# Operands of the top-k moved from SBUF to PSUM banks, and the place numbers of both token blocks made at once

## The chip, the cores and the metric

The kernel runs on one core of one Trainium2 chip. The metric is the device time of one launch in microseconds, the median of three runs. A profiled execution of the same program gives the trace that is read here. A core has five engines: TensorE (PE in the profile, its weight loads PEld), VectorE (DVE), ScalarE (ACT), GpSimd (POOL) and SyncE (SP), which here issues the transfers. On-chip memory is SBUF and, as TensorE's output, PSUM (8 banks of 512 float32 per partition).

## The reference

Two layers of an encoder trunk on 256 tokens of 1024 channels, float32. Each layer adds a mixed branch (attention, Hyena convolutions, FNet) and then a product-key expert branch, `x = x + peer(rmsnorm(x))`. The change lies in the expert branch:

```python
def peer(x, w_query, sub_keys, u_tab, v_tab):
    q = (xt @ w_query).reshape(T, PEER_HEADS, 2, PEER_DK // 2)           # T=256, 8 heads
    s = jnp.einsum('thpd,phkd->thpk', q, sub_keys)                       # 128 keys a side
    s_top, i_top = lax.top_k(s, PEER_TOPK)                               # 16 of 128, both sides
    cand = (s_top[:, :, 0, :, None] + s_top[:, :, 1, None, :]).reshape(T, 8, 256)
    cand_idx = (i_top[:, :, 0, :, None] * 128 + i_top[:, :, 1, None, :]).reshape(T, 8, 256)
    best, pos = lax.top_k(cand, PEER_TOPK)                               # 16 of 256
    idx = jnp.take_along_axis(cand_idx, pos, axis=-1)
    g = jax.nn.softmax(best, axis=-1)
    ...
    a = gelu(einsum('thkd,td->thk', u_tab[idx], xb))
    out = einsum('thk,thkd->td', g * a, v_tab[idx])
```

## The kernel before

The kernel doesn't gather experts. It multiplies all 16384 rows of the table u with the tokens (128 tiles of 128 experts), takes gelu, weighs the result by a gate matrix built from the picks, and multiplies it with all of the table v. Each layer runs in a loop over `l`; each engine has its own program, and the engines meet by semaphores (`Signal`, `at`).

Products are made in three parts for precision: each 128 x 1024 tile lands in `raw` (4 slots), ScalarE writes its rounded high part `tab_hi` and another engine the low part, `tab_lo = raw - tab_hi`, half a tile (128 x 512) at a time. `tab_hi` and `tab_lo` have two tile slots, four halves. A half may be written when TensorE has counted in `half_used` that it is through with the half two tiles earlier. TensorE's `u_tile` (L820 to L822) makes 12 matmuls of 256 columns for a half: high by x_lo, high by x_hi, low by x_hi, for 4 blocks of 128.

Who makes the low parts is written out by stages. For u tiles 0 to 39 it is GpSimd (`EARLY = 40`, `u_lower` in its program, L1264), since VectorE is then in the top-k. Tiles 40 to 47 are VectorE's (`u_lower_half`, L1592), in program order behind the top-k. When tile 47 is multiplied, TensorE waits for `topk_done`, transposes the picks (L868), waits for VectorE's copies of them (L1604 to L1606) and goes on with the stage of tiles 48 to 111, where the gates are built (L1611 to L1623) and GpSimd again makes the low parts. Behind `topk_done` GpSimd also sets parts of `work` to one (L1269 to L1278).

The top-k on VectorE, with tokens on the partitions and two token blocks `b` of 128:
- `top16` (L1543 to L1547) takes the 16 largest of a row in five passes: for the 16 rows (8 heads, 2 sides) of each block, giving `v_top` and `i_top`; L1555 turns the indices to float.
- For each block the candidate sums `cand` (L1558) of 16 x 16 for 8 heads, 2048 elements, and `top16` over them, giving `best` and `pos`.
- L1566 and L1567 subtract the largest from `best` (`best_done`), and ScalarE takes its exponential (L1118, `gate_exp`) at a place of its own order.
- For each block the place numbers: `pos >> 4` and `pos & 15` (L1571, L1572), turned to float (L1573), 128 elements for each of two sides. For each side the key look-up, each of 128 picks x 16 ranks = 2048 elements: compare with 0 to 15 (L1575), multiply by the key indices (L1580), sum over the ranks (L1581).
- After `gate_exp` the sum, the reciprocal and the product (L1583 to L1585, `topk_done`).

All these arrays lie in SBUF: `cand`, `eq` and `scores` in `work`, the others in `onehot`, `small` and `kc`. `link` lets VectorE wait for the instruction it wraps (`dve_step`, of which `DVE_STEPS` are counted in a layer), and `settled` drains the engine.

While this runs, TensorE writes PSUM banks 0 and 1 and ScalarE reads them (gelu). The picks' transposes go to banks 4 and 5.

Of the kernel before, what the change touches and what calls it, by code (L numbers as in the profile page):

```python
# [5 lines left out]
ALU = mybir.AluOpType  # L6
# [4 lines left out]
U32 = mybir.dt.uint32  # L11

P = 128
# [11 lines left out]
PH, KEYS, TOPK = 8, 128, 16  # L25
HP = 2 * PH
PICKS = PH * TOPK
# [38 lines left out]
QUERY_T = 0  # L66
UNIT_A = SPEC + 2048
SUBKEYS = SPEC
CAND, EQ, SCORES = 24576, 26624, 28672


A0, B0, O0, Q0, U0, V0, TILES = 0, 8, 16, 24, 40, 168, 296
# [7 lines left out]

FNET_BANKS, HYENA_BANKS, ATTN_BANKS = ((6, 7), (0, 2)), ((1, 4), (5, 3)), ((6, 7), (0, 2))
FNET_SUMS, HYENA_SUMS, ATTN_SUMS = 2, 4, 2
DVE_STEPS = 55
PARAM_MATS, PARAM_PIECES, DFT_PIECES = 2, 5, 6
FOLLOWING = 1 + PARAM_PIECES + DFT_PIECES + 1

# [8 lines left out]
def at(signal, layer, count):  # L95

    return signal.sem, layer * signal.per_layer + count


def hybrid_encoder(nc, x_in, w_proj, sub_keys, tab_u, tab_v, pvec, pmat, gain_qk, kconst, cfilter,  # L100
                   cdft, final_g, out):
    with ExitStack() as ctx:
# [3 lines left out]
        def sig(name, per_layer):  # L106
            return Signal(ctx.enter_context(nc.semaphore(name)), per_layer)
# [18 lines left out]
        ps = ctx.enter_context(nc.psum_tensor("ps", [P, 8, 512], F32))  # L126

        workf = work[:, :, :].rearrange("p j t -> p (j t)")
        onef = onehot[:, :, :, :, :].rearrange("p s a t c -> p (s a t c)")
# [3 lines left out]
        def area(start, n):  # L133
            return workf[:, start:start + n]
# [74 lines left out]
        subk = area(SUBKEYS, HP * KEYS).rearrange("p (k n) -> p k n", k=HP)  # L209
        scores = area(SCORES, TB * HP * KEYS).rearrange("p (b k n) -> p b k n", b=TB, k=HP)  # L210
        cand = area(CAND, PH * TOPK * TOPK).rearrange("p (h a b) -> p h a b", h=PH, a=TOPK)
        eq = area(EQ, PICKS * TOPK).rearrange("p (n r) -> p n r", r=TOPK)
        v_top = onef[:, 0:512].rearrange("p (b k n) -> p b k n", b=TB, k=HP)
        i_top = onef[:, 512:1024].bitcast(U32).rearrange("p (b k n) -> p b k n", b=TB, k=HP)
        i_topf = onef[:, 1024:1536].rearrange("p (b k n) -> p b k n", b=TB, k=HP)
        best = onef[:, 1536:1792].rearrange("p (b h n) -> p b h n", b=TB, h=PH)
        pos = onef[:, 1792:2048].bitcast(U32).rearrange("p (b n) -> p b n", b=TB)
        minus_j = chosenf[:, 0:SEQ]
        place_u = onef[:, 0:256].bitcast(U32).rearrange("p (s n) -> p s n", s=2)
        place_f = onef[:, 256:512].rearrange("p (s n) -> p s n", s=2)  # L220


        const_in = sig("const_in", 0)
# [11 lines left out]
        half_used = sig("half_used", 2 * TILES)  # L235
        dve_step = sig("dve_step", DVE_STEPS)
        mlp_ready = sig("mlp_ready", 2)
# [87 lines left out]
        def settled(eng):  # L325

            eng.drain()
# [958 lines left out]
        def _(dve):  # L1286
            v = nc.vector
# [4 lines left out]
            with dve.Fori(0, DEPTH) as l:  # L1292
                count = [0]

                def link(ins):

                    count[0] += 1
                    ins.then_inc(dve_step.sem, 1)
                    dve.wait_ge(*at(dve_step, l, count[0]))
# [240 lines left out]
                def top16(values, indices, row, rows):  # L1540


                    steps = (lambda r: v.max(values(r)[:, 0:8], row(r)),  # L1543
                             lambda r: v.max_index(indices(r)[:, 0:8], values(r)[:, 0:8], row(r)),
                             lambda r: v.match_replace(row(r), values(r)[:, 0:8], row(r), NEG),
                             lambda r: v.max(values(r)[:, 8:16], row(r)),
                             lambda r: v.max_index(indices(r)[:, 8:16], values(r)[:, 8:16], row(r)))  # L1547
                    for step in steps:
                        for r in range(rows):
                            last = step(r)  # L1550
                        settled(dve)

                for b in range(TB):
                    top16(lambda r: v_top[:, b, r, :], lambda r: i_top[:, b, r, :], lambda r: scores[:, b, r, :], HP)
                link(v.tensor_copy(i_topf, i_top))  # L1555
                for b in range(TB):
                    side = v_top[:, b, :, :].rearrange("p (h s) n -> p h s n", s=2)
                    v.tensor_tensor(  # L1558
                        cand, side[:, :, 0, :].rearrange("p h (n a) -> p h n a", a=1).broadcast_to([P, PH, 16, 16]),
                        side[:, :, 1:2, :].broadcast_to([P, PH, 16, 16]), ALU.add)  # L1560
                    settled(dve)
                    top16(lambda r: best[:, b, r, :], lambda r: pos[:, b, r * 16:(r + 1) * 16],
                          lambda r: cand[:, r, :, :].rearrange("p a b -> p (a b)"), PH)
# [3 lines left out]
                v.tensor_tensor(bests, bests, ssg.rearrange("p (n a) -> p n a", a=1).broadcast_to([P, 16, 16]),  # L1567
                                ALU.subtract).then_inc(best_done.sem, 1)

                for b in range(TB):  # L1570
                    link(v.tensor_single_scalar(place_u[:, 0, :], pos[:, b, :], 4, op=ALU.logical_shift_right))  # L1571
                    link(v.tensor_single_scalar(place_u[:, 1, :], pos[:, b, :], 15, op=ALU.bitwise_and))  # L1572
                    link(v.tensor_copy(place_f, place_u))  # L1573
                    for s in range(2):
                        link(v.tensor_tensor(  # L1575
                            eq, place_f[:, s, :].rearrange("p (n a) -> p n a", a=1).broadcast_to([P, PICKS, TOPK]),
                            iota16.rearrange("p (a n) -> p a n", a=1).broadcast_to([P, PICKS, TOPK]), ALU.is_equal))
                        side = i_topf[:, b, :, :].rearrange("p (h s) n -> p h s n", s=2)[:, :, s:s + 1, :]
                        eq4 = eq.rearrange("p (h k) r -> p h k r", h=PH)
                        link(v.tensor_tensor(eq4, eq4, side.broadcast_to([P, PH, TOPK, TOPK]), ALU.mult))  # L1580
                        link(v.tensor_reduce(chosen[:, s, b, :], eq, AX.X, ALU.add))  # L1581
# [247 lines left out]
```

## Time and profile before

| | us |
|---|---|
| median of 3 runs | 2042.25 (2041.79 to 2042.98) |
| profiled execution | 2039.95 |
| its span, first to last instruction | 2038.1 |
| TensorE busy (PE) | 1952.9 |
| VectorE busy (DVE) | 1320.5 |
| ScalarE busy (ACT) | 1103.7 |
| GpSimd busy (POOL) | 769.7 |

The busy time of an engine is an average over stages with different limits, so it says little of a change in one stage. Times in the views count from the span's start. In a timeline neighbouring instructions of one line are merged: the first number is the start, the second the time from the first start to the last end, xN the count. "out<-in" names the buffers; a bracket tells how long the engine was idle before and who released it. TensorE's matmuls overlap, so a single one is shown longer than the distance to its neighbour.

### The profile page before, as it was taken

The page shows a single profiled execution, that of the slowest core. Times are in us where ns is not written, and L with a number is a line of the kernel's source. Part 1 is how long each engine was busy: PE and PEld are TensorE (multiplying, and loading weights), DVE is VectorE, ACT ScalarE, POOL GpSimd, SP SyncE. Part 2 cuts the span into 40 slices and gives each one's busy share as a digit, 9 for nine tenths or more (in the row PEclk, how much of TensorE's full clock was granted, in tenths as well). Part 3 has the DMA queues.
Part 4 walks back from the last instruction along what each step waited for, and adds up shares of the span by engine and source line. Part 5 has one row for each costly group of instructions (what it writes and reads, how often), then busy time and mean ns, then how long its engine had stood idle before and what let it go on. Part 6 is the DMA issues. An engine that isn't in the chain of part 4 may idle for free.

```text
span 2038.1 us, 43068 instructions
## 1 busy us (share of the span) xinstructions
PE 1952.9 (96%) x12792; PEld 1782.5 (87%) x12792; DVE 1320.5 (65%) x2869; ACT 1103.7 (54%) x2124; POOL 769.7 (38%) x553
## 2 busy tenths in 40 slices
PE   7989998999999999999998999989999999999997
PEld 5779997999999888888777799979999998888886
DVE  4655699566666666666547557986666666666665
ACT  4344454666664555555533454546666555555554
POOL 4433599567770000000064416995767600000000
PEclk9989999999999999999989999999999999999999
DMA  6215454544445567555522154544444456665555
GB/s 210 74 42 172 151 184 138 162 137 141 137 140 172 186 208 246 196 192 191 184 74 83 55 183 148 183 144 145 144 134 144 134 175 196 226 227 194 196 192 179
DMA packets 93499, 327.09 MB, mean 160 GB/s; under 512 B 10736, under 2 KB 11504, under 8 KB 93168
## 3 DMA queue, kind: packets, MB, share of 16 engines
q1 hardware_dynamic: 93424, 326.18, 49.1%
q8 instruction: 36, 0.59, 0.1%
q14 instruction: 39, 0.32, 0.0%
HBM read 325.09 MB, written 1.05 MB: 160 GB/s over the span
## 4 chain that ended last, share of the span: by engine, by line
PE 89%; DVE 5%; issue 3%; POOL 2%; ACT 1%; DMA 0%; DVEq 0%; POOLq 0%; SPq 0%; ACTq 0%
PE ps L820 12%; PE ps L821 12%; PE ps L822 12%; PE ps L893 11%; PE ps L895 11%; PE ps L896 11%; PE ps L839 6%; PE ps L793 2%; PE ps L796 2%; PE ps L795 2%; POOL tab_lo L1264 1%; DVE work L1370 1%; PE ps L604 1%; PE ps L570 1%; PE ps L523 1%
## 5 line engine op out<-in xcount | busy, mean ns | idle before, releaser
L1264 POOL TENSOR_TENSOR tab_lo<-raw,tab_hi 128x512 fp32r<-128x512 f32 x416 | 585.9, 1422 | 262.5 <-ACT tab_hi L1096 181.6
L820 PE MATMUL ps<-x_lo,tab_hi 128*128 128x256 f32 x2048 | 591.8, 289 | 22.2 <-POOL tab_lo L1264 18.9
L822 PE MATMUL ps<-x_hi,tab_lo 128*128 128x256 f32 x2048 | 579.1, 283 | 0.0
L821 PE MATMUL ps<-x_hi,tab_hi 128*128 128x256 f32 x2048 | 579.0, 283 | 0.0
L1677 DVE TENSOR_TENSOR tab_lo<-raw,tab_hi 128x512 fp32r<-128x512 f32 x512 | 354.4, 692 | 268.7 <-ACT tab_hi L1191 265.3
L1096 ACT ACTIVATE tab_hi<-raw 128x512 fp32r<-128x512 f32 x504 | 317.6, 631 | 339.0 <-PE ps L822 334.5
L820 PEld LDWEIGHTS ps<-x_lo,tab_hi 128*128 128x128 f32 x2048 | 392.1, 191 | 25.7 <-POOL tab_lo L1264 25.5
L893 PE MATMUL ps<-tab_lo,w_hi 128*128 128x512 f32 x1024 | 398.6, 389 | 0.9 <-DVE w_lo L1685 0.9
L896 PE MATMUL ps<-tab_hi,w_lo 128*128 128x512 f32 x1024 | 398.4, 389 | 0.0
L895 PE MATMUL ps<-tab_hi,w_hi 128*128 128x512 f32 x1024 | 398.4, 389 | 0.0
L821 PEld LDWEIGHTS ps<-x_hi,tab_hi 128*128 128x128 f32 x2048 | 392.6, 192 | 0.0
L822 PEld LDWEIGHTS ps<-x_hi,tab_lo 128*128 128x128 f32 x2048 | 392.0, 191 | 0.0
L1191 ACT ACTIVATE tab_hi<-raw 128x512 fp32r<-128x512 f32 x512 | 319.3, 624 | 89.8 <-PE ps L896 89.0
L893 PEld LDWEIGHTS ps<-tab_lo,w_hi 128*128 128x128 f32 x1024 | 192.2, 188 | 41.8 <-DVE tab_lo L1677 1.7
L896 PEld LDWEIGHTS ps<-tab_hi,w_lo 128*128 128x128 f32 x1024 | 192.2, 188 | 39.7
L895 PEld LDWEIGHTS ps<-tab_hi,w_hi 128*128 128x128 f32 x1024 | 192.2, 188 | 39.7
L1181 ACT ACTIVATE w_hi<-work 128x256 fp32r (+1 forms) x256 | 106.8, 417 | 201.7 <-PE ps L896 200.3
L1623 DVE TENSOR_TENSOR work<-ps,work 128x512 f32 (+1 forms) x128 | 88.5, 692 | 157.4 <-PE ps L839 157.4
L1212 POOL TENSOR_TENSOR small<-small,kc 128x2 f32<-128x2 f32 x10 | 6.9, 691 | 445.8 <-DVE small L1304 428.6
L920 ACT ACTIVATE tab_hi<-raw 128x512 fp32r<-128x512 f32 (+1 forms) x168 | 100.3, 609 | 130.6 <-PE ps L796 47.3
L1611 DVE TENSOR_SCALAR onehot<-kc,picks 128x128 f32<-128x128 f32 x512 | 168.1, 389 | 0.6
L1219 POOL TENSOR_TENSOR tab_lo<-raw,tab_hi 128x512 fp32r<-128x512 f32 (+1 forms) x96 | 121.4, 1277 | 116.9 <-ACT tab_hi L920 115.5
(204 smaller groups left out, 2524.8 us busy)
## 6 DMA issues: line engine op xcount, KB each, us to landing
raw<-tab_u SPq DMA_DIRECT2D x256, 512.0 KB, 3.3
raw<-tab_v SPq DMA_DIRECT2D x256, 512.0 KB, 3.3
raw<-w_proj SPq DMA_DIRECT2D x68, 512.0 KB, 3.6
raw<-w_proj SPq DMA_DIRECT2D x16, 384.0 KB, 3.2
work<-cdft SPq DMA_DIRECT2D x18, 256.0 KB, 3.8
work<-cfilter SPq DMA_DIRECT2D x9, 256.0 KB, 4.3
work<-sub_keys SPq DMA_DIRECT2D x2, 1024.0 KB, 6.5
work<-pmat SPq DMA_DIRECT2D x6, 304.0 KB, 4.4
```

What stands on the lines that cost most here:

```text
L820: mm(bank, hi, x_lo[:, 4 * h + k, :], start=(h + k == 0), stop=False)
L821: mm(bank, hi, x_hi[:, 4 * h + k, :], start=False, stop=False)
L822: last = mm(bank, lo, x_hi[:, 4 * h + k, :], start=False, stop=(h + k == 4))
L839: last = mm(ps[:, 2 + s, t * P:(t + 1) * P], onehot[:, s % 2, 0, t, :], onehot[:, s % 2, 1, t, :], start=True, stop=True)
L893: mm(bank, w_hi[:, s % 2, tok], lo, start=(first and s == 0), stop=False, skip_group_check=True)
L895: mm(bank, w_hi[:, s % 2, tok], hi, start=False, stop=False, skip_group_check=True)
L896: last = mm(bank, w_lo[:, s % 2, tok], hi, start=False, stop=last_tile, skip_group_check=True)
L1096: fn(half(tab_hi, s, h), half(raw, s, h), ACT.Copy).then_inc(hi_done.sem, 1)
L1191: fn(half(tab_hi, s, h), half(raw, s, h), ACT.Copy).then_inc(hi_done.sem, 1)
L1264: tt(half(tab_lo, s, h), half(raw, s, h), half(tab_hi, s, h).bitcast(F32), ALU.subtract).then_inc(lo_pool.sem, 1)
L1611: last = v.tensor_scalar(onehot[:, slot, 0, t, :], iota, picks[:, 0, bass.ds(n * 4 + t, 1)], picks[:, 2, bass.ds(n * 4 + t, 1)], ALU.is_eq ...
L1677: v.tensor_tensor(half(tab_lo, s, h), half(raw, s, h), half(tab_hi, s, h).bitcast(F32), ALU.subtract).then_inc(lo_dve.sem, 1)
```

## The change

The `eq` array leaves SBUF for PSUM banks 4 to 7 (2048 float32), so that the compare writes it there, the multiply reads and writes it there, and the reduce reads it there. The float place numbers `place_f` lie in bank 3, and are made for both blocks at once: one shift, one mask, each of 256 elements, and one conversion of 512, in place of two rounds of 128, 128 and 256. `place_u` takes 512 words of `onehot`, where `v_top` lay. A new copy puts the first side's 16 best key scores of all heads and blocks, 256 elements, in bank 2 (`v_first`), and the candidate sums read them from there, the other side from SBUF. `DVE_STEPS` goes from 55 to 51.

```diff
-CAND, EQ, SCORES = 24576, 26624, 28672
+CAND, SCORES = 24576, 28672
-DVE_STEPS = 55
+DVE_STEPS = 51
-        eq = area(EQ, PICKS * TOPK).rearrange("p (n r) -> p n r", r=TOPK)
-        place_u = onef[:, 0:256].bitcast(U32).rearrange("p (s n) -> p s n", s=2)
-        place_f = onef[:, 256:512].rearrange("p (s n) -> p s n", s=2)
+        posf = onef[:, 1792:2048].bitcast(U32)
+        place_u = onef[:, 0:512].bitcast(U32).rearrange("p (s n) -> p s n", s=2)
+
+        v_first = ps[:, 2, 0:256].rearrange("p (m n) -> p m n", n=TOPK)
+        place_f = ps[:, 3, :].rearrange("p (s n) -> p s n", s=2)
+        eq = ps[:, 4:8, :].rearrange("p k c -> p (k c)").rearrange("p (n r) -> p n r", r=TOPK)
...
+                v.tensor_copy(v_first, v_top.rearrange("p b (h s) n -> p s (b h) n", s=2)[:, 0, :, :])
                 link(v.tensor_copy(i_topf, i_top))
                 for b in range(TB):
                     side = v_top[:, b, :, :].rearrange("p (h s) n -> p h s n", s=2)
                     v.tensor_tensor(
-                        cand, side[:, :, 0, :].rearrange("p h (n a) -> p h n a", a=1).broadcast_to([P, PH, 16, 16]),
-                        side[:, :, 1:2, :].broadcast_to([P, PH, 16, 16]), ALU.add)
+                        cand, v_first[:, b * PH:(b + 1) * PH, :].rearrange("p h (n a) -> p h n a", a=1)
+                        .broadcast_to([P, PH, 16, 16]), side[:, :, 1:2, :].broadcast_to([P, PH, 16, 16]), ALU.add)
...
+                v.tensor_single_scalar(place_u[:, 0, :], posf, 4, op=ALU.logical_shift_right)
+                link(v.tensor_single_scalar(place_u[:, 1, :], posf, 15, op=ALU.bitwise_and))
+                link(v.tensor_copy(place_f, place_u))
                 for b in range(TB):
-                    link(v.tensor_single_scalar(place_u[:, 0, :], pos[:, b, :], 4, op=ALU.logical_shift_right))
-                    link(v.tensor_single_scalar(place_u[:, 1, :], pos[:, b, :], 15, op=ALU.bitwise_and))
-                    link(v.tensor_copy(place_f, place_u))
                     for s in range(2):
+                        place = place_f[:, s, b * PICKS:(b + 1) * PICKS]
                         link(v.tensor_tensor(
-                            eq, place_f[:, s, :].rearrange("p (n a) -> p n a", a=1).broadcast_to([P, PICKS, TOPK]),
+                            eq, place.rearrange("p (n a) -> p n a", a=1).broadcast_to([P, PICKS, TOPK]),
                             iota16.rearrange("p (a n) -> p a n", a=1).broadcast_to([P, PICKS, TOPK]), ALU.is_equal))
                         side = i_topf[:, b, :, :].rearrange("p (h s) n -> p h s n", s=2)[:, :, s:s + 1, :]
                         eq4 = eq.rearrange("p (h k) r -> p h k r", h=PH)
                         link(v.tensor_tensor(eq4, eq4, side.broadcast_to([P, PH, TOPK, TOPK]), ALU.mult))
                         link(v.tensor_reduce(chosen[:, s, b, :], eq, AX.X, ALU.add))
```

## Rows read from the trace of the kernel before

**Rows 1.** The page: the chain that ended last, shares of the span.
```profile
PE 89%; DVE 5%; issue 3%; POOL 2%; ACT 1%; DMA 0%; DVEq 0%; POOLq 0%; SPq 0%; ACTq 0%
```

**Rows 2.** GpSimd's line L1264: durations in ns; who waited, us, times.
```profile
L1264 POOL TENSOR_TENSOR tab_lo<-raw,tab_hi x416: 1264/1296/3320, 216.3 to 1623.8; 128x512 fp32r<-128x512 f32 x139
...
  PE ps L820: 18.9, 14
```

**Rows 3.** Busy by stretch: length, engines' busy us (instructions), clock, DMA share, GB/s.
```profile
228.00:300.00 72.00, 72.00 (x601) 71.89 (x601) 69.39 (x361) 38.57 (x63) 65.38 (x48) 1.00 0.50 166
300.00:314.00 14.00, 14.00 (x119) 14.00 (x118) 13.64 (x35) 7.29 (x12) 13.46 (x11) 1.00 0.60 200
314.00:352.00 38.00, 28.55 (x225) 27.13 (x224) 37.41 (x18) 16.76 (x27) 38.00 (x19) 1.00 0.36 115
352.00:377.50 25.50, 25.50 (x214) 25.50 (x214) 11.70 (x17) 13.10 (x22) 14.45 (x7) 1.00 0.63 199
```

**Rows 4.** Timeline of TensorE: the stage's first product and end, both layers.
```profile
227.75 0.36 PE L820 MATMUL ps<-x_lo,tab_hi 128*128 128x256 f32 x1
...
377.52 0.82 PE L868 MATMUL ps<-kc,chosen 128*128 128x128 f32 x6
...
1237.93 0.36 PE L820 MATMUL ps<-x_lo,tab_hi 128*128 128x256 f32 x1
...
1387.68 0.82 PE L868 MATMUL ps<-kc,chosen 128*128 128x128 f32 x6
```

**Rows 5.** Timeline of VectorE, first layer: place numbers, first compare, end of top-k.
```profile
308.37 1.32 DVE L1571 TENSOR_SCALAR onehot<-onehot 128x128 uint32<-128x128 uint32 x1
...
311.31 3.27 DVE L1575 TENSOR_TENSOR work<-onehot,kc 128x2048 f32<-128x2048 f32 x1
...
329.29 1.36 DVE L1571 TENSOR_SCALAR onehot<-onehot 128x128 uint32<-128x128 uint32 x1
...
333.27 3.27 DVE L1575 TENSOR_TENSOR work<-onehot,kc 128x2048 f32<-128x2048 f32 x1
...
351.98 0.81 DVE L1585 TENSOR_TENSOR chosen<-onehot,small 128x256 f32<-128x256 f32 x1
353.30 2.73 DVE L1592 TENSOR_TENSOR tab_lo<-raw,tab_hi 128x512 fp32r<-128x512 f32 x4 [0.50 <-PE ps L822]
...
384.03 0.69 DVE L1623 TENSOR_TENSOR work<-ps,work 128x512 f32<-128x512 f32 x1 [1.46 <-PE ps L839]
```

**Rows 6.** Timeline of GpSimd: beside a compare, a reduce and a gate's product.
```profile
312.42 3.30 POOL L1264 TENSOR_TENSOR tab_lo<-raw,tab_hi 128x512 fp32r<-128x512 f32 x1
...
318.96 1.30 POOL L1264 TENSOR_TENSOR tab_lo<-raw,tab_hi 128x512 fp32r<-128x512 f32 x1
...
383.61 1.29 POOL L1264 TENSOR_TENSOR tab_lo<-raw,tab_hi 128x512 fp32r<-128x512 f32 x1 [3.92 <-ACT tab_hi L1096]
```

**Rows 7.** VectorE's groups by line and shape: busy us, mean ns, idle before.
```profile
L1623 DVE TENSOR_TENSOR work<-ps,work 128x512 f32 x112 | 77.4, 691 | 140.4 <-PE ps L839 140.4
L1575 DVE TENSOR_TENSOR work<-onehot,kc 128x2048 f32<-128x2048 f32 x8 | 26.8, 3350 | 0.3
L1580 DVE TENSOR_TENSOR work<-work,onehot 128x2048 f32<-128x2048 f32 x8 | 26.0, 3248 | 0.3
...
L1581 DVE TENSOR_REDUCE chosen<-work 128x128 f32<-128x2048 f32 x8 | 18.3, 2286 | 0.3
...
L1558 DVE TENSOR_TENSOR work<-onehot 128x2048 f32<-128x2048 f32 x4 | 12.5, 3123 | 0.2
...
L1699 DVE TENSOR_TENSOR x<-ps,x 128x1024 f32<-128x1024 f32 x4 | 4.9, 1224 | 4.2 <-PE ps L896 4.0
```

**Rows 8.** Timeline of ScalarE: the exponential of the best scores.
```profile
317.02 0.42 ACT L1118 ACTIVATE onehot<-onehot 128x256 f32<-128x256 f32 x1
```

**Rows 9.** ScalarE's groups by line and shape: gelu in place and into SBUF.
```profile
L1127 ACT ACTIVATE ps<-ps 128x512 f32<-128x512 f32 x80 | 46.4, 580 | 3.9 <-PE ps L822 3.9
...
L1100 ACT ACTIVATE work<-ps 128x512 f32 x40 | 23.2, 579 | 0.0
```

## The prediction

> **What bounds the kernel now.** I began with the page's shares of the chain that ended last: TensorE holds 89% of it and VectorE 5% [rows 1]. So a shorter VectorE stretch is worth nothing in itself; it counts only where TensorE stands still because of it. The view of GpSimd's line L1264, which makes the low part of a half tile, shows that TensorE's first product of a half (L820) waited for it for 18.9 us in 14 places, although the median half takes GpSimd only 1.296 us [rows 2]. The longest takes 3.320 us. That gap is the thing to explain. GpSimd's name for this in the page is POOL, VectorE's DVE.
>
> The table by stretch says where it sits. From 228 to 314 us TensorE starts 601 + 119 matmuls in 86 us, one each 0.12 us. From 314 to 352 us it starts 225 in 38 us, where 317 would fit at that pace; then it is at pace again [rows 3]. The granted clock is 1.00 (the 2.4 GHz level) in all four stretches, so the missing 92 matmuls (11.0 us) are no matter of the clock. The whole stage of the first 48 table tiles is 48 x 2 halves x 12 = 1152 matmuls, 138.24 us at 0.12. It starts at 227.75 and the transposes behind it start at 377.52, that is 149.77 us: 11.5 us lost. The second layer has the same from 1237.93 to 1387.68, 149.75 us [rows 4]. The waits account for 18.9 / 2 = 9.5 us of it in a layer; the rest fits the product that comes first after a stop, which takes 0.36 us where in the stream one follows the other by 0.12 [rows 2, 4].
>
> The timelines of VectorE and GpSimd side by side say why. In just this stretch, from 311.31 us on, VectorE runs the key look-up: compare (L1575) 3.35 us in the mean, multiply (L1580) 3.25, reduce (L1581) 2.29, each four times a layer [rows 5, 7]. GpSimd's half that meets the first compare takes 3.30 us (there are eight like it in a layer, one for each compare and multiply), the one beside the first reduce 1.30 us [rows 6]. The reduce streams the same 2048 elements, from one SBUF operand, in 2286 ns [rows 7]. So the two engines do not merely share the memory: an instruction of VectorE with two SBUF operands and one of GpSimd take turns. A compare is 1 us of waiting for GpSimd's half to end and 2.3 us of own work, in which GpSimd stands, 3.30 - 1.28 = 2.02 us. Eight of those per layer are 16.2 us of GpSimd, of which TensorE feels 11.5; some 4.7 us go into the up to four halves that GpSimd may be ahead, and into its 0.15 us of reserve per half (1.29 against TensorE's 12 x 0.12 = 1.44). The two candidate sums of a layer (L1558, 3.12 us in the mean) do the same earlier, before 300 us, and TensorE loses nothing there, by the count above [rows 3, 7].
>
> **The part of GpSimd.** After the change compare, multiply and candidate sum each have one operand in PSUM and one in SBUF. The nearest row for that is the gate's product (L1623, one PSUM operand, one in SBUF): at 384.03 us it runs for 0.69 us inside a GpSimd half of 1.29 us, and neither is longer for it; in 112 of them the mean is 691 ns [rows 5 to 7]. The chance that a two-operand instruction with a PSUM operand no longer takes turns rests on that row and on the reduce. Then GpSimd needs 1.26 to 1.30 us a half against 1.44, and TensorE keeps its pace [rows 2]. Worth per layer: up to 11.5 us, of which I leave 0.2 for the longer first product and small delays: 11.3. The page "SBUF — State Buffer" of the Trainium skill, section "Who interferes with whom", says the same: two SBUF inputs contend with a GpSimd instruction that reads SBUF, at most one does not; by it too the whole wait would go.
>
> **The part of VectorE, and the cover.** TensorE's tiles 40 to 47 are lowered by VectorE, in its program behind the top-k. If GpSimd stops being late, this is what is late next. TensorE would ask for tile 40's first half at 227.75 + 80 x 1.44 + 0.1 = 343.0 us. Now the top-k ends at 351.98 + 0.81 = 352.8 and the first lowered half is there at 353.30 + 2.73 / 4 = 354.0, 1.2 us after [rows 5]. So the top-k has to end by 341.8: 11.0 us sooner than now, or TensorE only changes what it waits for. The sum for one layer:
> - Candidate sums: 2 x 3.12 become 2 x 2.29. The price of 2048 elements with one PSUM operand is from 691 ns for 512 (L1623) and 1224 for 1024 (L1699), so 1.04 ns an element and 2.29 us; equal to the SBUF reduce. Saves 1.67. Added is the copy of 256 key scores to PSUM, 0.691 - 256 x 0.00104 = 0.42 us. Net 1.2 [rows 7].
> - Place numbers: now two rounds, from 308.37 to 311.31 and from 329.29 to 333.27, 6.9 us. After: one shift and one mask of 256 elements and one copy of 512 into PSUM. A shift of 128 elements takes 1.32 us, where 128 at 1.04 ns with the fixed part of 0.16 would be 0.3: mostly turns with GpSimd, which I keep, 2 x 1.3; a copy of 512 with a PSUM operand takes 0.69. Together 3.3, so it saves 3.6 (2.7 if all three are 1.4, 5.4 if the shifts meet nothing) [rows 5, 7].
> - Compares: 4 x 3.35 = 13.4 become 9.2: 4.2. Multiplies: 4 x 3.25 = 13.0 become 9.2: 3.8. Reduces: 2.29 from SBUF, 2.29 by the slope from PSUM: unchanged [rows 7].
>
> In all 12.9 us: the top-k ends at 339.9, 1.9 us before it must. ScalarE's exponential, for which VectorE waits before its last three instructions, is done at 317.02 + 0.42 = 317.4 and hangs on ScalarE's own place in the order [rows 8]. The raw tiles arrive while TensorE is at pace (166 to 200 GB/s), so the pace asks of the DMA queues what they already do [rows 3]. GpSimd's setting of ones follows the top-k and ends earlier by as much.
>
> What no row shows is VectorE writing to PSUM: compare, multiply and two copies now do. Lower bound is the SBUF price, 2.29 us. The nearest row of a write is ScalarE's, whose gelu from PSUM takes 580 ns in place (L1127) against 579 into SBUF (L1100) [rows 9]. The dearest that I can argue is that the multiply and compare take two passes, 4.4 us each (2 x 2.13 + 0.15). I take 2.29, the row nearest. The page "VectorE: DVE Perf Modes", section on the TRN2 errata, speaks against the change: 120 cycles of fixed cost from PSUM against 58 from SBUF. The trace does not have it: 512 elements take 691 ns with a PSUM operand (L1623) and 2.73 / 4 = 0.68 us with SBUF operands alone (L1592) [rows 5, 7]. By the page, at 65 ns in each of some 16 instructions, the top-k would end 1.0 us later, at 340.9, still in time, with half the margin: the sum would not move, and rival 1 would be twice as near.
>
> **The sum.** 2 layers x 11.3 = 22.6 us. The profiled execution took 2039.95 us (span 2038.1); it would take 2017.35 (span 2015.5). The median of the runs is 2.3 above the profiled one, so the median goes from 2042.25 to 2019.65. Nothing behind the stage gives it back: the gate stage begins when the picks are transposed, on TensorE's time, and everything after is a chain of its own.
>
> **The rivals.**
> 1. VectorE is late at tile 40. It decides from the point where the eight compares and multiplies take 1.9 / 8 = 0.24 us more than 2.29. At the present 3.3 us each (no gain in length, but no turns for GpSimd either), the top-k ends 8.1 us later, TensorE waits 6.2 of it and 2 x 5.1 remain: 2032. For it: the margin is thin, and no row shows such a write. Against it: ScalarE's row.
> 2. The other side, slower. If a read and a write of PSUM by the same instruction take two passes (4.4 us), the top-k ends 8 x 2.1 = 16.9 us later, TensorE stands at tile 40 for 15.0 us, and loses 15.0 - 11.3 = 3.7 us a layer: 2049.6. From 2.29 + (1.9 + 11.3) / 8 = 3.94 us per instruction the change is a loss. Against it: L1127, in place.
> 3. Half of the turns stay (the multiplies, say, since they read and write the same tensor). GpSimd stands 8.1 us a layer, 4.7 of it are absorbed as now, 3.4 reach TensorE, and 2 x 7.9 are won: 2026.5.
> 4. The change does not do what it says: GpSimd stands as long as now, for a reason other than the second SBUF operand. Then the place numbers still get shorter, on an engine that isn't waited for: 2042. Against it: the reduce and L1623.
>
> **How the numbers follow.** Forecast 0.74, 2018.5 to 2021.5 by itself. Rivals 1 and 3, which end between 2022 and 2036, 0.15 together. Rival 4, 0.06. Rival 2, 0.05. The range reaches from 2017.0 (all of the 11.5 us, and some spread of the runs) to 2029.0, which takes in rival 3 and rival 1 up to 3.1 us an instruction. A measurement of this kernel can tell about 0.2% (4 us) from no change: faster 0.89, same 0.06, slower 0.05.
>
> **What the profile after would show.** L1264's longest half on GpSimd under 2 us and no wait of TensorE for it; about 0.12 us per matmul through the whole stage, and 138.5 to 139 us from its first product to the transposes. Compare, multiply and candidate sum near 2.29 us each; the top-k's last instruction near 340 us. If the compares are longer than 2.6 us and TensorE waits for VectorE's lowering at tile 40, rival 1 or 2 is at work; if GpSimd still shows halves of 3.3 us, rival 3 or 4. The prediction is wrong if a write to PSUM by VectorE has a price of its own or if a PSUM operand doesn't end the turns.

## The result, and the profile after

The changed kernel takes 2019.55 us (median of 4 runs, 2018.87 to 2020.94) against 2042.02 for the kernel before measured beside it: ratio 0.9893, 95% interval 0.9879 to 0.9907. The forecast was 2019.65. The profiled execution took 2020.94 us, its span is 2019.0 (2038.1 before).

The busy table by stretch of the changed kernel, over the same stage as [rows 3] (start and end of the stretch, its length, the busy us and instruction counts of PE, PEld, DVE, ACT and POOL, granted clock, share and GB/s of the transfers):

```profile
230.00:302.00 72.00, 72.00 (x602) 72.00 (x602) 69.71 (x365) 38.58 (x64) 63.14 (x49) 1.00 0.52 169
302.00:316.00 14.00, 14.00 (x119) 14.00 (x119) 13.69 (x31) 6.95 (x12) 12.77 (x11) 1.00 0.55 186
316.00:354.00 38.00, 38.00 (x319) 38.00 (x318) 32.02 (x23) 22.99 (x37) 33.19 (x21) 1.00 0.56 186
354.00:368.00 14.00, 14.00 (x119) 14.00 (x118) 4.85 (x7) 6.89 (x13) 3.43 (x3) 1.00 0.52 171
```

The third stretch is the one that matters: 319 matmuls in 38 us where there were 225 (a count in brackets takes in every instruction that lies in the stretch with any part, so it is a little higher than the number of starts). GpSimd, which had no free moment in those 38 us, is now busy for 33.2. The timeline of TensorE gives the stage's length, to be set against [rows 4]:

```profile
229.38 0.36 PE L823 MATMUL ps<-x_lo,tab_hi 128*128 128x256 f32 x1
...
367.69 0.49 PE L871 MATMUL ps<-kc,chosen 128*128 128x128 f32 x3
...
1230.23 0.36 PE L823 MATMUL ps<-x_lo,tab_hi 128*128 128x256 f32 x1
...
1368.54 0.82 PE L871 MATMUL ps<-kc,chosen 128*128 128x128 f32 x6
```

138.31 us in either layer, against 149.77 and 149.75, and 138.24 for 1152 matmuls at 0.12. So nothing is left to win in this stage without fewer or shorter matmuls. GpSimd's line (durations in ns, lowest, median, longest; then who waited, us, times) is now L1267, and no product of TensorE waits for it, only two weight loads (PEld):

```profile
L1267 POOL TENSOR_TENSOR tab_lo<-raw,tab_hi x416: 1264/1296/1799, 217.9 to 1604.6; 128x512 fp32r<-128x512 f32 x139
...
  PEld ps L823: 3.7, 2
```

The median is that of [rows 2] and the longest fell from 3320 to 1799 ns. VectorE's groups by shape (xcount, busy us, mean ns), for [rows 7]:

```profile
L1580 DVE TENSOR_TENSOR ps<-ps,kc 128x2048 f32<-128x2048 f32 x8 | 18.4, 2300 | 0.3
L1585 DVE TENSOR_TENSOR ps<-ps,onehot 128x2048 f32<-128x2048 f32 x8 | 18.4, 2299 | 0.3
L1586 DVE TENSOR_REDUCE chosen<-ps 128x128 f32<-128x2048 f32 x8 | 18.3, 2291 | 0.3
...
L1562 DVE TENSOR_TENSOR work<-ps,onehot 128x2048 f32<-128x2048 f32 x4 | 9.2, 2291 | 0.2
```

and its timeline from the index conversion to the first lowered half of tile 40, for [rows 5]:

```profile
270.66 0.43 DVE L1558 COPY ps<-onehot 128x256 f32<-128x256 f32 x1
271.00 1.26 DVE L1559 CAST onehot<-onehot 128x512 f32<-128x512 uint32 x1
...
309.82 1.39 DVE L1574 TENSOR_SCALAR onehot<-onehot 128x256 uint32<-128x256 uint32 x1
...
313.27 2.30 DVE L1580 TENSOR_TENSOR ps<-ps,kc 128x2048 f32<-128x2048 f32 x1
...
341.99 0.42 DVE L1590 TENSOR_TENSOR chosen<-onehot,small 128x256 f32<-128x256 f32 x1
342.92 1.90 DVE L1597 TENSOR_TENSOR tab_lo<-raw,tab_hi 128x512 fp32r<-128x512 f32 x3 [0.50 <-ACT tab_hi L1099]
```

From the stage's first product to the end of the top-k it was 352.79 - 227.75 = 125.0 us; now it is 342.41 - 229.38 = 113.0. The first half of tile 40 is there at 342.92 + 1.90 / 3 = 343.55, and TensorE asks for it, by its pace of 1.44 us a half, at 229.38 + 80 x 1.44 + 0.1 = 344.7: a margin of 1.1 us.

### The profile page after: what moved, and what is told of

It is laid out like the page before. It is cut to its first block, busy times and chain, and to the rows that moved or that the text cites. A ratio compares the mean times of both kernels' runs of the same rounds, so it can differ in the third digit from the quotient of the medians.

```text
span 2019.0 us, 43056 instructions
## 1 busy us (share of the span) xinstructions
PE 1950.9 (97%) x12792; PEld 1783.7 (88%) x12792; DVE 1299.6 (64%) x2865; ACT 1103.6 (55%) x2124; POOL 736.6 (36%) x553
## 4 chain that ended last, share of the span: by engine, by line
PE 91%; DVE 4%; issue 2%; ACT 1%; DMA 0%; POOL 0%; DVEq 0%; POOLq 0%; SPq 0%; ACTq 0%
PE ps L823 12%; PE ps L824 12%; PE ps L825 12%; PE ps L898 11%; PE ps L896 11%; PE ps L899 11%; PE ps L842 6%; PE ps L796 2%; PE ps L799 2%; PE ps L798 2%; DVE work L1373 1%; PE ps L607 1%; PE ps L573 1%; PE ps L526 1%; PE ps L528 1%
## 5 line engine op out<-in xcount | busy, mean ns | idle before, releaser
L1267 POOL TENSOR_TENSOR tab_lo<-raw,tab_hi 128x512 fp32r<-128x512 f32 x416 | 552.5, 1337 | 270.9 <-ACT tab_hi L1099 183.2
```

Source lines behind the costliest of these rows:

```text
L1267: tt(half(tab_lo, s, h), half(raw, s, h), half(tab_hi, s, h).bitcast(F32), ALU.subtract).then_inc(lo_pool.sem, 1)
```

## The experiments

The theory: VectorE's instructions with two SBUF inputs and GpSimd's take turns, TensorE loses what GpSimd is late, and the end of the top-k has to stay ahead of tile 40. Four kernels take the change apart, two load the cover, and the rest carry the step to other places; one run repeats the changed kernel beside them. "Stage" is TensorE's time from the first product of the 48 tiles to the transposes, read as above.

**The place numbers alone**, all operands in SBUF (added to the kernel before):

```diff
+        place_u = onef[:, 0:512].bitcast(U32).rearrange("p (s n) -> p s n", s=2)
+        place_f = area(CAND, 512).rearrange("p (s n) -> p s n", s=2)
...
+                v.tensor_single_scalar(place_u[:, 0, :], posf, 4, op=ALU.logical_shift_right)
+                link(v.tensor_single_scalar(place_u[:, 1, :], posf, 15, op=ALU.bitwise_and))
+                link(v.tensor_copy(place_f, place_u))
                 for b in range(TB):
-                    link(v.tensor_single_scalar(place_u[:, 0, :], pos[:, b, :], 4, op=ALU.logical_shift_right))
...
```

> The kernel before with the place numbers of both blocks made at once, every operand left in SBUF. Theory (GpSimd is held up by VectorE's instructions with two SBUF inputs, and TensorE by GpSimd): the compares and multiplies still hold GpSimd eight times a layer, so the stage of the first 48 tiles still takes 149.7 us and the time stays at 2042 us (2040.5 to 2043.5), although the top-k ends some 3.5 us sooner. Rival (it is the length of VectorE's work that counts): 3.5 us a layer won, 2035 us.

Measured: 2043.8 us, ratio 1.0008 (0.9999 to 1.0018), stage 150.1 us. That is 0.3 us above the range and far from the rival's 2035. The top-k ended 2.5 us sooner after the stage's start (350.95 - 228.44 = 122.5 us, where some 3.5 sooner was expected), and it was worth nothing. The group of the compare and the wait of TensorE for GpSimd (us, times, longest) are as before the change:

```profile
L1577 DVE TENSOR_TENSOR work<-work,kc 128x2048 f32<-128x2048 f32 x8 | 27.1, 3386 | 0.3
```
```profile
PE ps L821 <- POOL tab_lo L1265: 19.7, 14, 1.6
```

So VectorE's length was not what bound the stage.

**The PSUM operands alone**, the place numbers made per block again (in the changed kernel):

```diff
-                v.tensor_single_scalar(place_u[:, 0, :], posf, 4, op=ALU.logical_shift_right)
...
+                for b in range(TB):
+                    link(v.tensor_single_scalar(place_u[:, 0, :], pos[:, b, :], 4, op=ALU.logical_shift_right))
```

> The changed kernel with the place numbers made block by block again, the operands in PSUM kept. Theory: GpSimd is free of VectorE, no half above 2 us; the top-k ends about 2.6 to 3.6 us later than in the changed kernel, where the first half of tile 40 was there 1.1 us before TensorE asked, so TensorE waits 1.5 to 2.5 us per layer for VectorE's lowering at tile 40: 2022.5 to 2024.5 us. Rival (the place numbers are of no account once GpSimd is free): 2019.5 us.

Measured: 2023.11 us (2020.55 to 2023.39), ratio 0.9905 (0.9888 to 0.9922), stage 139.5 us. A new wait is there, small and once a layer, for VectorE's low part of tile 40:

```profile
PE ps L822 <- DVE tab_lo L1595: 1.8, 2, 0.9
```

The top-k ended at 344.75 - 229.65 = 115.1 us after the stage's start, 2.1 later than in the changed kernel (2.6 to 3.6 were expected); less the margin of 1.1 this is 1.0, and the stage is 1.2 longer. The two stages explain 2.4 us; that the medians lie 3.6 apart is not explained by them, and the two intervals overlap. The place numbers are worth something only because the PSUM operands are there.

**Input or output?** Two kernels each leave one of the look-up's two long instructions with two SBUF inputs. In the first `eq` is back in SBUF: the compare reads PSUM and writes SBUF. In the second only the place numbers are: the compare reads SBUF twice and writes PSUM.

```diff
-        eq = ps[:, 4:8, :].rearrange("p k c -> p (k c)").rearrange("p (n r) -> p n r", r=TOPK)
+        eq = area(26624, PICKS * TOPK).rearrange("p (n r) -> p n r", r=TOPK)
```

> The changed kernel with the array eq back in SBUF: the compare still reads its place numbers from PSUM but writes to SBUF, the multiply has two SBUF inputs again. Theory (the second SBUF input holds GpSimd): compares 2.29 us and no hold, multiplies 3.25 us and four halves of 3.3 us per layer; TensorE loses about 3.4 us a layer, 2026.5 us (2024 to 2029). Rival (it is the output in SBUF that holds GpSimd): compares hold it too, eight halves of 3.3 us, near 2042 us.

```diff
-        place_f = ps[:, 3, :].rearrange("p (s n) -> p s n", s=2)
+        place_f = area(CAND, 512).rearrange("p (s n) -> p s n", s=2)
```

> The changed kernel with the float place numbers back in SBUF: the compare has two SBUF inputs but still writes to PSUM, the multiply is as changed. Theory (inputs decide): compares 3.3 us and four halves of 3.3 us per layer, multiplies 2.30 us without a hold; TensorE loses about 3.4 us a layer, 2026.5 us (2024 to 2029). Rival (the output decides): no long half, 2019.5 us.

Measured: 2026.93 us (ratio 0.9929, 0.9910 to 0.9948) and 2026.80 us (0.9925, 0.9908 to 0.9941), stages 142.1 and 142.1 us. VectorE's groups, first of the one with `eq` in SBUF, then of the one with the place numbers there:

```profile
L1585 DVE TENSOR_TENSOR work<-work,onehot 128x2048 f32<-128x2048 f32 x8 | 20.6, 2579 | 0.3
L1580 DVE TENSOR_TENSOR work<-ps,kc 128x2048 f32<-128x2048 f32 x8 | 18.3, 2291 | 0.3
```
```profile
L1580 DVE TENSOR_TENSOR ps<-work,kc 128x2048 f32<-128x2048 f32 x8 | 20.7, 2590 | 0.3
L1585 DVE TENSOR_TENSOR ps<-ps,onehot 128x2048 f32<-128x2048 f32 x8 | 18.4, 2299 | 0.3
```

Of these two-operand instructions it doesn't matter which it is, nor where it writes: the one with two SBUF inputs is held, the one with one is not. GpSimd's longest half is 3325 and 3326 ns in these kernels. That is half of the turns for a third of the loss (3.8 us of 11.5 a layer); the sum of the prediction, in which GpSimd's lead takes up 4.7 us of standing, gives 3.4. The held instruction is at 2.58 us in the mean shorter than before the change (3.25). With `eq` in SBUF the first multiply of a layer takes 3.16 us and the other three 2.38 to 2.40: these begin when a GpSimd half is nearly over, and wait 0.1 us. GpSimd has four long halves in the layer all the same, of 3.16 to 3.33 us.

The second of these kernels also answers the question for a short instruction with one SBUF input, the conversion of the place numbers. In both rows here it begins 0.1 us behind the start of a GpSimd half; first the changed kernel, which writes to PSUM, then the one that writes to SBUF:

```profile
312.54 0.70 DVE L1576 CAST ps<-onehot 128x512 f32<-128x512 uint32 x1
```
```profile
312.86 1.48 DVE L1576 CAST work<-onehot 128x512 f32<-128x512 uint32 x1
```

Here the output decides: written to PSUM it doesn't wait, written to SBUF it waits for the half's end (314.05 us) and is done 0.3 us after it.

**The candidate sums back in SBUF**, with the copy left out:

```diff
-                v.tensor_copy(v_first, v_top.rearrange("p b (h s) n -> p s (b h) n", s=2)[:, 0, :, :])
...
-                        cand, v_first[:, b * PH:(b + 1) * PH, :].rearrange("p h (n a) -> p h n a", a=1)
+                        cand, side[:, :, 0, :].rearrange("p h (n a) -> p h n a", a=1)
```

> The changed kernel with the candidate sums reading both operands from SBUF again, without the copy to PSUM. Theory: each sum holds one GpSimd half at 3.1 to 3.3 us, twice a layer near 272 and 290 us, which GpSimd's lead takes up, so TensorE does not wait for it; the top-k ends 0.4 to 1.3 us later, against a margin of 1.1 us at tile 40. Stage 138.3 to 138.6 us, time 2019.5 to 2020.5 us. Rival (every hold reaches TensorE in part): 0.7 of 2 x 2 us a layer, 2025 us.

Measured: 2019.96 us, ratio 0.9891 (0.9876 to 0.9906), stage 138.48 us. GpSimd has a half of 3.29 and one of 3.15 us beside the sums, and TensorE doesn't feel them. The top-k ends 340.88 - 227.68 = 113.2 us after the stage's start, 0.2 later than in the changed kernel: the third part of the change shortens VectorE by 0.2 us, and is worth nothing that can be measured, as [rows 3] already said of the sums.

**The cover, loaded.** Three, and in another kernel two, more compares in the changed kernel, which have one operand in PSUM and change no value:

```diff
+                        for _ in range(4 if b + s == 2 else 1):
...
```

> The changed kernel with the third compare of the key look-up made four times, which changes no value: three more instructions of 2.33 us a layer that have one operand in PSUM. Theory (TensorE needs the top-k's end at tile 40, and GpSimd is not held by these): 7.0 us more of VectorE, less the margin of 1.1, is 5.9 us of waiting for VectorE's lowering per layer, stage 144.2 us, time 2031.3 us (2030 to 2033), no GpSimd half above 2 us. Rival (the end of the top-k is covered by more than the margin that I read): below 2026 us.

> The changed kernel with the third compare made three times: two more instructions of 2.33 us a layer. With three more TensorE stood 5.85 us at tile 40, and its granted clock was 0.50 for some 6 us afterwards, which cost another 2.6 us a layer. Theory A (any stop of some length at this place brings the clock down): a stop of 4.67 less 1.1, 3.6 us, stage 138.3 + 3.6 + 2.6 = 144.5 us, time 2031.8 us. Theory B (a stop of 3.6 us is short enough to keep the clock, as those of 1.6 us in the kernel before were): stage 141.9 us, time 2026.7 us.

Measured: three more, 2038.37 us, ratio 0.9978 (0.9968 to 0.9987), stage 146.8 us. Two more, 2032.34 us, ratio 0.9945 (0.9930 to 0.9960), stage 143.6 us. The waits came out as worked out, 5.85 and 3.5 us, and the ends of the stages did not: with three more 144.2 us and a time of at most 2033 were expected. The waits of TensorE, its timeline around the stop and the busy table by stretch, with three more:

```profile
PE ps L823 <- DVE tab_lo L1598: 11.7, 2, 5.8
```
```profile
350.51 0.58 PE L823 MATMUL ps<-x_lo,tab_hi 128*128 128x256 f32 x1 [5.85 <-DVE tab_lo L1598]
350.89 0.41 PE L824 MATMUL ps<-x_hi,tab_hi 128*128 128x256 f32 x1
...
355.59 0.41 PE L825 MATMUL ps<-x_hi,tab_lo 128*128 128x256 f32 x1
```
```profile
344.00:350.00 6.00, 0.67 (x6) 0.46 (x4) 5.36 (x6) 1.11 (x2) 0.66 (x2) 0.93 0.00 1
350.00:351.00 1.00, 0.49 (x2) 0.49 (x3) 1.00 (x3) 0.00 (x0) 1.00 (x1) 0.50 0.00 0
351.00:352.00 1.00, 1.00 (x7) 1.00 (x7) 1.00 (x3) 0.00 (x0) 1.00 (x1) 0.50 0.00 0
...
355.00:356.00 1.00, 1.00 (x7) 1.00 (x7) 0.00 (x0) 0.00 (x0) 1.00 (x1) 0.53 0.70 287
356.00:358.00 2.00, 2.00 (x19) 2.00 (x18) 0.69 (x1) 1.14 (x2) 2.00 (x2) 1.00 0.03 12
```

The same table with two more:

```profile
346.00:348.00 2.00, 0.00 (x0) 0.00 (x0) 1.43 (x4) 0.00 (x0) 0.89 (x2) 1.00 0.00 0
348.00:350.00 2.00, 1.72 (x11) 1.72 (x12) 2.00 (x4) 0.00 (x0) 2.00 (x1) 0.81 0.00 0
350.00:352.00 2.00, 2.00 (x12) 2.00 (x11) 0.73 (x2) 0.63 (x1) 2.00 (x1) 0.50 0.87 277
352.00:354.00 2.00, 2.00 (x16) 2.00 (x16) 0.38 (x1) 0.64 (x1) 2.00 (x1) 0.84 0.74 248
```

The column to read is the one behind the last bracket, the granted clock. When TensorE goes on after the stop of 5.85 us it is 0.50 (the 1.2 GHz level), and stays there for some 5 us. The first product takes 0.38 us, and from 350.89 to 355.80 there are 23 at 0.213 us each in place of 0.12: 0.26 + 23 x 0.093 = 2.4 us. That is all but 0.2 of the part of the stage that the stop doesn't explain, 146.8 - 138.3 - 5.85 = 2.6 us. After the stop of 3.5 us the low stretch is shorter, and the part is 143.6 - 138.3 - 3.5 = 1.8 us. Theory B of the second run is out, and theory A had the cost 0.8 us a layer too high. The margin of 1.1 us is confirmed: each compare is one for one a wait behind it (7.0 - 1.1 = 5.9, 4.7 - 1.1 = 3.6).

**The same step in other stages.** The convolution's second and third taps (12 instructions a layer) read the channels from the banks in which TensorE left them; a signal keeps TensorE from writing bank 0 too early:

```diff
-                        last = v.scalar_tensor_tensor(conv[:, c, :], p_t[:, c, tap:tap + 256], par("cw", 6 * tap + c),
-                                                      conv[:, c, :], ALU.mult, ALU.add)
+                    last = v.scalar_tensor_tensor(conv[:, c, :], ps[:, c // 2, (c % 2) * 256:(c % 2) * 256 + 256],
+                                                  par("cw", 6 + c), conv[:, c, :], ALU.mult, ALU.add)
...
```

> The changed kernel, with the same step made in another stage: the second and third tap of the Hyena short convolution (12 instructions of 256 elements a layer, both tensor inputs in SBUF, 0.98 us each while GpSimd lowers) read the channels from TensorE's PSUM banks. Theory: each takes 0.42 to 0.48 us, the convolution ends some 6 us sooner, and the 2.7 us per layer that TensorE waits for it shrink to at most 0.5: 2014.5 to 2016 us. Rival (the time given back there is lost at the next wait, since TensorE's products of that stage wait for something else anyway): 2019.5 us.

Measured: 2011.72 us (2011.27 to 2014.08), ratio 0.9848 (0.9834 to 0.9861). The group before (both taps, in the changed kernel) and after (the second tap):

```profile
L1373 DVE SCALAR_TENSOR_TENSOR work<-work,pv 128x256 f32<-128x256 f32 x24 | 21.9, 980 | 0.1
```
```profile
L1375 DVE SCALAR_TENSOR_TENSOR work<-ps,pv,work 128x256 f32<-128x256 f32 x12 | 4.9, 476 | 0.1
```

The third tap's 12 instructions take 0.476 us each as well. TensorE's wait for the convolution (2.7 us a layer) is gone from its list. The gain of 7.8 us is larger than the 5.4 of the wait. The traces show a part of it: the first layer's stage of the 48 tiles begins at 225.97 us here, at 229.38 in the changed kernel and at 227.87 in its repetition; and from that stage's end to the second layer's start it is 859.2 us here, 862.5 and 861.8 in the other two. That makes 6.7 us against the first trace and 4.5 against the second. 1.5 us of what these two differ by comes from TensorE's clock. Both stop for 2.7 us before L589, and behind it, from 75 to 79 us, the first has a granted clock of 0.65 (the column behind the last bracket) and the second, the very same kernel, of 1.00:

```profile
75.00:79.00 4.00, 3.79 (x16) 3.80 (x17) 0.15 (x1) 1.12 (x2) 0.97 (x1) 0.65 0.47 135
```
```profile
75.00:79.00 4.00, 3.62 (x21) 3.52 (x22) 0.33 (x1) 1.65 (x3) 1.22 (x2) 1.00 0.47 135
```

Over the eleven traces of this study that have this stop, twice each, the clock fell behind it 9 times of 22. Where it fell, the next long stop came some 1.5 us later (31.8 us behind this one for 30.3). So the step saves the stop and also what the clock takes now and then. How much of the median's gain is of which was not tried apart, and about 1 us of it is within what the runs differ by.

The cosine part of the rotary product, written to PSUM banks:

```diff
+        rope_cos = ps[:, 4:7, :].rearrange("p k c -> p (k c)")[:, 0:1280]
...
-                v.tensor_tensor(rope3, qn3, cos_g, ALU.mult)
+                v.tensor_tensor(rope_cos.rearrange("p (b n) -> p b n", b=TB), qn3, cos_g, ALU.mult)
...
-                v.tensor_tensor(rope, rope, rot, ALU.add).then_inc(rope_done.sem, 1)
+                v.tensor_tensor(rope, rope_cos, rot, ALU.add).then_inc(rope_done.sem, 1)
```

> The changed kernel, with the rotary product by the cosines written to PSUM banks 4 to 6, so that the sum of 1280 elements behind it reads one operand there. Theory: the sum takes 1.49 us in place of 2.43, TensorE's wait for it of 3.4 us per layer becomes 2.5, and 1.9 us are won in two layers: 2017.7 us. The product itself keeps its two SBUF inputs and its 2.03 us. Rival (the wait is handed on to the next one): 2019.5 us.

Measured: 2017.17 us, ratio 0.9874 (0.9859 to 0.9889). The sum takes 1.49 us in place of 2.43, and TensorE's wait for it went from 3.4 to 2.4 us a layer. The intervals of this kernel and the changed one overlap, so it is the trace that shows the gain, not the time.

```profile
L1496 DVE TENSOR_TENSOR work<-ps,onehot 128x1280 f32<-128x1280 f32 x2 | 3.0, 1491 | 0.1
```

Both steps together, and both with the second block's queries in PSUM as well, with the changed kernel beside them:

> The changed kernel once more, beside the three below on the same chip: 0.9893 of the kernel before, 2019.5 us (2018.5 to 2021), stage of the first 48 tiles 138.3 us.

> The changed kernel with both steps: the convolution's second and third tap read PSUM (it won 7.8 us alone), and the rotary product's cosine part lies in PSUM (2.4 us alone). Theory (two separate places of the chain): the gains add up, 2019.5 - 10.2 = 2009.3 us (2008 to 2011). Rival (one gain hides the other, since both end at the same wait): 2011.7 us.

```diff
+        qn_of = (qn[:, 0:640], ps[:, 4:8, :].rearrange("p k c -> p (k c)")[:, 1280:1920])
...
-            src = qn[:, b * 640:(b + 1) * 640].rearrange("p (h a e d) -> p h a e d", h=10, a=2, e=2)
+            src = qn_of[b].rearrange("p (h a e d) -> p h a e d", h=10, a=2, e=2)
```

> As the kernel with both steps, and the second block's normalised queries and keys lie in PSUM too, so that its two crossed products (320 elements, 1.35 us each beside GpSimd) read one operand from there; the cosine product is made block by block. Theory: the two take 0.49 us each, 1.7 us less per layer, of which the split product gives back at most 0.2; 3.0 us in two layers: 2006.3 us (2005.5 to 2008.5). Rival (the crossed product of GpSimd, which runs beside it, ends last): 2009.3 us.

Measured: the changed kernel 2020.40 us, ratio 0.9894 (0.9878 to 0.9909), as before. Both steps 2012.26 us, ratio 0.9846 (0.9833 to 0.9860): no better than the taps alone. All three 2006.64 us (2004.77 to 2007.15), ratio 0.9820 (0.9806 to 0.9833), the fastest kernel of the study. Of the missing gain in the second the traces say that the wait for the sum did get shorter (3.4 to 2.4 us a layer), and the two intervals leave room for 1.9 us, so it is undecided rather than refuted: the span of its trace is 1.5 us shorter than that of the taps alone, the median is not. The third won 5.6 us over the second where 3.0 were expected. The waits of TensorE for the sum, and the busy table of the first layer's attention stage, with both steps and then with all three:

```profile
PE ps L673 <- DVE work L1502: 4.9, 2, 2.4
```
```profile
98.00:104.00 6.00, 3.55 (x25) 3.31 (x24) 4.77 (x4) 2.00 (x6) 4.40 (x3) 0.90 0.07 12
104.00:110.00 6.00, 6.00 (x39) 5.67 (x38) 5.51 (x10) 3.66 (x6) 0.00 (x0) 0.81 0.20 76
110.00:120.00 10.00, 7.07 (x26) 5.75 (x24) 6.42 (x11) 6.17 (x25) 0.00 (x0) 0.66 0.00 0
```
```profile
PE ps L674 <- DVE work L1504: 1.5, 2, 0.8
```
```profile
98.00:104.00 6.00, 5.24 (x43) 4.87 (x41) 4.38 (x8) 3.48 (x9) 3.45 (x3) 1.00 0.20 55
104.00:110.00 6.00, 4.82 (x25) 3.75 (x24) 5.93 (x10) 3.17 (x8) 0.00 (x0) 1.00 0.08 32
110.00:120.00 10.00, 7.58 (x37) 6.45 (x38) 5.27 (x10) 5.58 (x22) 0.00 (x0) 0.83 0.00 0
```

With the wait at 0.8 us in place of 2.4 the granted clock stays at 1.00 up to 110 us, where it was 0.90 and 0.81. The traces divide the gain of 2.8 us a layer. TensorE goes on after its next long stop (L698, now L699) at 112.42 us in place of 114.04, 1.6 sooner, which is the shorter wait; the stage of the 48 tiles begins at 222.49 in place of 225.30, 2.8 sooner. So 1.2 us (1.1 in the second layer) are won behind that stop, and in the 8 us behind it the granted clock is 0.66 and then 0.91, where it was 0.50 and 0.77. That the clock brings all of these 1.2 us fits its size but was not tried apart.

## Why the prediction was right, step by step

- What bounds the stage: right. TensorE waited for GpSimd and GpSimd for VectorE's instructions with two SBUF inputs. The place numbers alone won nothing; taking the second input away won it all, whichever side the output was on.
- GpSimd's part: 11.3 us a layer were forecast, 11.46 and 11.44 measured. The 0.2 held back for delays weren't needed.
- A write to PSUM by VectorE, for which no row stood: 2.30 us for 2048 elements, the lower bound. Rivals 1 and 2, which needed 0.24 and 1.65 us more, fell with it. The larger fixed cost for PSUM that the Trainium skill states ("VectorE: DVE Perf Modes", section on the TRN2 errata) isn't there either: the reduce takes 2291 ns from PSUM and 2286 from SBUF.
- The end of the top-k: 12.9 us sooner was forecast, 12.0 measured, and the margin at tile 40 was 1.1 us, not 1.9. The eight compares and multiplies came out as worked out. What was mis-sized is the short instructions that still meet GpSimd: the index conversion (L1559) went from 0.43 to 1.26 us, since it now begins 0.3 us behind the start of a GpSimd half, where it began just ahead of one; the copy of 16 elements (L1570) went from 0.98 to 1.31, and the place numbers took 3.45 us in place of 3.3; the last product (L1590) got shorter, 0.42 for 0.81. The sum had kept their old durations, though each depends on when it starts. So the candidate sums with their copy, forecast to shorten VectorE by 1.2 us, shortened it by 0.2, as the kernel without them showed.
- Place numbers: forecast as 3.6 us of VectorE; without them the top-k ended 2.1 us later when the operands are in PSUM. Their loss costs 1.2 us a layer of stage when the operands are in PSUM, and nothing when they are not.
- Rival 3 (half of the turns) was priced at 3.4 us a layer, 2026.5 us; the two kernels that make it real lost 3.8 and gave 2026.9 and 2026.8.
- Rivals 1 and 2 were priced too low. They counted TensorE's stop alone: for 6.2 us of it rival 1 has 2032, and the kernel with a stop of 5.85 us took 2038.4, 2.6 us a layer of it by the lower clock. No run had rival 2's stop of 15 us; by the same reckoning it would have ended above the 2049.6 that was written.
- The total: 22.6 us forecast, 22.5 measured between the medians, 22.9 by the two stages. That the time came out within 0.1 us of the forecast is luck, since single runs of one kernel differ by 2 to 4 us here. The two profiled executions differ by 19.0 us only. The missing 3.8 us lie outside the stage: its first product comes 1.6 us later than before (229.38 for 227.75), and the stretch between the two layers' stages takes 2.1 us more (862.5 for 860.4). The trace of the kernel before is one in which the clock held behind stops where it falls in others: behind the 2.7 us stop of the convolution in both layers, and behind the second layer's stop of 3.4 us for the rotary sum, where it fell in 20 of the 22 cases that the traces have. That is worth about 3.0 of the 3.8 us, and the change touches none of these places.

## What to carry to other kernels

Where VectorE and GpSimd work side by side, look first at the longest instruction of GpSimd, not the mean: a half of 3.3 us beside a median of 1.3 shows the turns, and one operand of VectorE's instruction in a free PSUM bank ends them, at no price for the long instructions in this case (a conversion of 512 elements that didn't wait took 0.43 us from SBUF to SBUF and 0.70 to PSUM). Then ask what is late next, and load that cover with a known amount of work to measure it; here it was 1.1 us. And a shorter instruction is worth only what the engine that waits for it gains: 2.5 us less of VectorE won nothing alone.

## What the runs showed of the hardware

- For an instruction with two tensor inputs the turns depend on the number of SBUF inputs, not on the output: reading SBUF twice and writing PSUM holds GpSimd (longest half 3326 ns), reading PSUM and SBUF and writing SBUF does not (2291 ns).
- Short copies, shifts and conversions with one SBUF input and an SBUF output also wait beside GpSimd: a copy of 16 elements took 0.98 and 1.31 us in two kernels, a shift of 256 uint32 1.39 us, of 128 between 0.70 and 1.36, a conversion of 512 elements 0.43 us, or 1.26 and 1.48 where it met a GpSimd half. With its output in PSUM the conversion took 0.70 us inside a GpSimd half.
- In the stage of the 48 tiles, stops of TensorE up to 1.6 us left the granted clock at 1.00; after 3.5 and 5.85 us it was 0.50 for a while, which cost 1.8 and 2.6 us beyond the stop.
- The same stop of 2.7 us in the convolution was followed by a fall of the clock in 9 of 22 cases, at some 1.5 us each; of two traces of the very same kernel one shows such a fall in its first layer and the other none. Two traces can differ by that much with no change of the program.
